# Variances ahead of the bonus products, attention scaled tile by tile, and part of w_out's operand splits ahead of the meeting

## The reference, cut to what matters

```python
def rwkv7_time_mix(...):            # 6 heads of 64
    ...
    _, y = lax.scan(step, s0, xs)   # the recurrence over 1024 tokens
    ym = y.mean(-1, keepdims=True)
    yv = jnp.square(y - ym).mean(-1, keepdims=True)
    yn = ((y - ym) * lax.rsqrt(yv + GN_EPS)).reshape(B, S, RWKV_WIDTH) * lnx_g + lnx_b
    bonus = (jnp.sum(r_h * k_h * r_k, -1, keepdims=True) * v_h).reshape(B, S, RWKV_WIDTH)
    return ((yn + bonus) * g).astype(zb.dtype)

def hybrid_mixer(...):
    ...
    o_a = rms_norm(o_a, attn_norm_g)          # attention, width 384
    o_b = rwkv7_time_mix(...)                 # width 384
    o_c = multiscale_pool(zc, pool_w, pool_scale)   # width 256
    return jnp.concatenate([o_a, o_b, o_c], axis=-1) @ w_out
```

## Time and profile before

| | us |
|---|---|
| median of three runs | 3576.71 (3575.73 to 3585.78) |
| the profiled execution, its own time | 3576.34 |
| its span | 3574.3 |
| TensorE busy | 3274.0 (92%) |
| VectorE busy | 1913.2 (54%) |
| ScalarE busy | 1053.9 (29%) |
| GpSimd busy | 1146.4 (32%) |

### The profile page before, as it was taken

The page is one execution under the profiler, slowest core; times in us unless marked ns, Lnnn a source line. Parts: engine busy times, 40 slices in busy tenths (PEclk is TensorE's granted clock), DMA queues, the critical chain, the costliest instruction groups (busy, mean ns, idle before and its releaser), DMA issues.

```text
span 3574.3 us, 61403 instructions
## 1 busy us (share of the span) xinstructions
PE 3274.0 (92%) x23080; PEld 2373.5 (66%) x23080; DVE 1913.2 (54%) x3061; ACT 1053.9 (29%) x1857; POOL 1146.4 (32%) x952
## 2 busy tenths in 40 slices
PE   7989967999999999999989998689899999999997
PEld 3444435876577888888735444368675788888884
DVE  5788996444623333333467899854526133333335
ACT  3333334442212211211235343344402111221212
POOL 1175632641212222222114755155222122222221
PEclk9999979999999999999999899799999999999998
DMA  3110000001111111111111001000011111111111
GB/s 123 45 33 21 29 23 6 0 1 36 48 36 48 47 47 47 53 47 48 40 55 33 28 24 33 11 6 0 7 31 58 42 51 49 47 47 47 48 46 47
DMA packets 43861, 132.72 MB, mean 37 GB/s; under 512 B 9280, under 2 KB 11840, under 8 KB 43072
## 3 DMA queue, kind: packets, MB, share of 16 engines
q1 hardware_dynamic: 37280, 122.41, 10.5%
q10 hardware_dynamic: 6432, 8.40, 0.9%
HBM read 117.15 MB, written 5.24 MB: 34 GB/s over the span
## 4 chain that ended last, share of the span: by engine, by line
PE 59%; DVE 14%; issue 10%; DVEq 10%; POOLq 2%; ACT 1%; POOL 1%; DMA 1%; PEldq 0%; ACTq 0%; SPq 0%; PEld 0%
DVE M L1715 8%; DVEq L1719 8%; PE wide L1087 7%; PE bank L1089 7%; PE bank L1087 7%; PE bank L1088 7%; PE wide L1089 7%; PE wide L1088 7%; PE wide L799 3%; DVE PB L1735 2%; PE wide L629 2%; PE bank L799 2%; POOLq L1591 1%; DVE WK L1717 1%; DVEq L1716 1%
## 5 line engine op out<-in xcount | busy, mean ns | idle before, releaser
L1590 POOL TENSOR_TENSOR WL<-WR,WH 128x1024 fp32r<-128x1024 f32 x160 | 403.1, 2519 | 1479.2 <-ACT WH L1385 1478.5
L669 PE MATMUL wide<-X,WR 128*128 128x512 f32 (+1 forms) x1088 | 504.7, 608 | 11.6 <-ACT X L1144 9.4
L1385 ACT ACTIVATE WH<-WR 128x1024 fp32r<-128x1024 f32 x160 | 168.2, 1053 | 735.6 <-PE bank L1089 430.2
L2019 DVE TENSOR_TENSOR RB<-RB 128x512 f32<-128x512 f32 x128 | 88.5, 692 | 549.0 <-ACT RB L1411 549.0
L669 PEld LDWEIGHTS wide<-X,WR 128*128 128x128 f32 x1088 | 202.7, 196 | 246.9 <-issue 220.9
L1715 DVE MAX8 M<-WK 128x8 f32<-128x512 f32 (+5 forms) x342 | 314.9, 921 | 23.7
L1717 DVE MATCH_REPLACE8 WK<-M,WK 128x512 f32<-128x512 f32 (+5 forms) x342 | 309.5, 905 | 1.2 <-issue 1.2
L1087 PE MATMUL wide<-XH,WH 128*128 128x512 f32 x640 | 261.6, 409 | 18.1 <-POOLq L1591 9.5
L1087 PE MATMUL bank<-XH,WH 128*128 128x512 f32 x640 | 255.7, 400 | 0.0
L1089 PE MATMUL wide<-XH,WL 128*128 128x512 f32 x640 | 252.8, 395 | 0.0
L1088 PE MATMUL wide<-XL,WH 128*128 128x512 f32 x640 | 252.5, 395 | 0.0
(11 more groups left out here) (318 smaller groups left out, 6399.2 us busy)
## 6 DMA issues: line engine op xcount, KB each, us to landing
WR<-in_w SPq DMA_DIRECT2D x128, 512.0 KB, 3.5
WR<-in_w_in SPq DMA_DIRECT2D x34, 512.0 KB, 3.5
WR<-in_w_out SPq DMA_DIRECT2D x16, 512.0 KB, 3.5
WR<-in_w_gate SPq DMA_DIRECT2D x16, 512.0 KB, 5.5
Y<-in_xT SPq DMA_DIRECT2D x2, 2048.0 KB, 13.3
out_T<-X SPq DMA_DIRECT2D x1, 4096.0 KB, 11.1
QZS<-QZ ACTq DMA_DIRECT2D x48, 64.0 KB, 2.0
QZS<-QZ ACTq DMA_DIRECT2D x64, 48.0 KB, 1.9
```

The lines of the kernel that those rows point to most:

```text
L669: mm = e.matmul(BK_[hf][:, 0:q.stop - q.start], WR[:, i % RING, kt, :], X[:, kt, q], start=kt == 0, stop=kt == KT - 1)
L1385: e.activation(WH[:, split_seq(i) % 2, :, :], WR[:, i % RING, :, :], ACT.Copy).then_inc(w_high, 1)
L1590: e.tensor_tensor(WL[:, s, :, :], WR[:, i % RING, :, :], WH[:, s, :, :].bitcast(F32), ALU.subtract)
L2019: e.tensor_tensor(RB[:, b, :], RB[:, b, :], RB[:, b, :], ALU.mult).then_inc(square_ready, 1)
```

## The change

The tail and the first steps of the projection are ordered anew.
- `var` moves ahead of all `bonus` entries in `post_seq`, and its matmuls take each half slab as soon as it is squared. Bonus 1 and 2 move behind the spreads; VectorE's list follows.
- ScalarE makes the copies for bonus 1 and 2 together behind the last squares.
- `scale_attention` works on one tile of 128 tokens and runs in `rwkv_tile`, between the last `XS` and the first `MT` of each tile.
- The slabs are taken in the order `M_ORDER` = 6, 0, 1, 2, 3, 4, 5, 7. The high parts of four of them (one pooling, three attention), the low parts of two and both parts of w_out's first block are made ahead of meeting 2; `LOW_AT` says where a low part lies in `ML`.
- Two pads move `G4` and the weights' high and low parts in SBUF, so that what is now written early lies on nothing that is still in use.

```diff
+M_ORDER = [6, 0, 1, 2, 3, 4, 5, 7]
+M_EARLY, M_AHEAD = 4, 2
+LOW_AT = [3, 4, 5, 0, 1, 2, 6, 7]
+G4_PAD, W_PAD = 4109, 819
...
+        sb("under_g4", [P, G4_PAD], post)
         G4 = sb("G4", [P, 3, S], post)
...
+        sb("under_wh", [P, W_PAD], m)
         WH = sb("WH", [P, 2, KT, P], m, F32R)
...
-        post_seq = [("mean", 0), ("mean", 1), ("mean", 2), ("bonus", 0), ("var", 0), ("bonus", 1), ("bonus", 2),
-                    ("spread", 0), ("spread", 1), ("gate", 0), ("spread", 2), ("gate", 1), ("gate", 2)]
+        post_seq = [("mean", 0), ("mean", 1), ("mean", 2), ("var", 0), ("bonus", 0), ("spread", 0), ("spread", 1),
+                    ("bonus", 1), ("gate", 0), ("spread", 2), ("bonus", 2), ("gate", 1), ("gate", 2)]
...
+            def variances(L):
+                for i in range(NP):
+                    for hf in range(2):
+                        e.wait_ge(y_sq, L * 6 + (2 * i + hf + 1))
+                        bank = post_bank(("var", 0), hf)
...
+                            mm = e.matmul(bank[:, c:c + 2], G1[:, i, q:q + P], block_ones[:, 0:P:HD],
...
-                post_read(e, L, ("gate", 0), 0)
+                post_read(e, L, ("spread", 2), 0)
                 keep_clock(2, 4)
                 meet(e, L, 2)
...
                     dense(mt, ZW + mt, lambda kt: kt, MH, ML,
...
+                          if mt == 0 else None, order=M_ORDER, low_at=LOW_AT)
...
+                def split_mixed(L, n0, n1):
+                    for kt in M_ORDER[n0:n1]:
+                        if kt < NP:
+                            e.wait_ge(att_scaled, L * NB + NB)
+                            e.wait_ge(bonus_in, L * 3 + (kt + 1))
+                        e.activation(MH[:, kt, :], mixed[kt], ACT.Copy).then_inc(m_high, 1)
...
+                    for k in ((0,), (), (1, 2))[i]:
+                        e.activation(G3[:, k, :], BZ[:, BR + k, :], ACT.Copy, scale=par_col("rk", k))\
+                         .then_inc(bonus_half, 1)
+                split_mixed(L, 0, 2)
                 split_high(L, ZW)
...
+                split_mixed(L, 2, M_EARLY)
...
                 meet(e, L, 2)
+                split_mixed(L, M_EARLY, KT)
...
                     e.tensor_tensor(G3[:, i, :], G3[:, i, :], BZ[:, BK + i, :], ALU.mult).then_inc(bonus_in, 1)
+                split_low(ZW)
                 meet(e, L, 2)
...
-            def scale_attention():
+            def scale_attention(t):
+                q = tile_columns(t)
                 for p in range(3):
...
+                    ins = e.scalar_tensor_tensor(A3[:, p, q], A3[:, p, q], par_col("ag", p), RSD[:, q], ALU.mult, ALU.mult)
+                ins.then_inc(att_scaled, 1)
...
                 for i in range(NP):
                     centre(i)
-                bonus(0)
-                scale_attention()
-                for i in range(1, NP):
-                    bonus(i)
+                lows(0, M_AHEAD)
                 for hf in range(2):
                     post_read(e, L, ("var", 0), hf)
...
                 e.reciprocal(g2, g2).then_inc(y_rstd, 1)
+                bonus(0)
                 normalise(0)
                 normalise(1)
+                bonus(1)
                 gated(0)
                 normalise(2)
+                bonus(2)
                 gated(1)
                 gated(2)
                 meet(e, L, 2)
-                for kt in range(KT):
...
+                lows(M_AHEAD, KT)
```

More of the change, by code:

```diff
@@ L971, in head_sums @@
                 return mm
+            def variances(L):
[3 more added lines that the diff above has]
+                        bank = post_bank(("var", 0), hf)
+                        for t in range(NB // 2):
+                            c, q = (i * (NB // 2) + t) * 2, hf * HALF + t * P
+                            mm = e.matmul(bank[:, c:c + 2], G1[:, i, q:q + P], block_ones[:, 0:P:HD],
+                                          start=True, stop=True)
+                        if i == NP - 1 and hf == 0:
+                            mm.then_inc(post_full, 1)
+                return mm
             def head_spread(bank, values, i, hf):
@@ L1058, in _ @@
                         if what == "var":
-                            e.wait_ge(y_sq, L * 6 + (2 * (NP - 1) + hf + 1))
-                            mm = head_sums(post_bank((what, i), hf), G1, hf)
+                            if hf == 0:
+                                variances(L).then_inc(post_full, 1)
+                            continue
                         elif what == "spread":
@@ L1070, in _, with dense @@
                         mm.then_inc(post_full, 1)
-                post_read(e, L, ("gate", 0), 0)
+                post_read(e, L, ("spread", 2), 0)
                 keep_clock(2, 4)
                 meet(e, L, 2)
-                def dense(n, i, ws, high, low, kts=KT, f=0, ready=None, halves=(0, 1)):
+                def dense(n, i, ws, high, low, kts=KT, f=0, ready=None, halves=(0, 1), order=range(KT), low_at=range(KT)):
                     e.wait_ge(w_low, L * N_SPLIT + f * N_F + (split_seq(i) + 1))
@@ L1082, in dense @@
                         e.wait_ge(d_free[b], L * D_USES + f * (N_DENSE // 2) + (n // 2 + 1))
-                        for kt in range(kts):
+                        for k, kt in enumerate(order[:kts]):
                             if ready:
-                                ready(kt, hf)
+                                ready(k, hf)
                             w, q = ws(kt), hs(hf)
-                            e.matmul(BK_[b], WH[:, s, w, :], high[:, kt, q], start=kt == 0, stop=False)
-                            e.matmul(BK_[b], WH[:, s, w, :], low[:, kt, q], start=False, stop=False)
-                            mm = e.matmul(BK_[b], WL[:, s, w, :], high[:, kt, q], start=False, stop=kt == kts - 1)
+                            e.matmul(BK_[b], WH[:, s, w, :], high[:, kt, q], start=k == 0, stop=False)
+                            e.matmul(BK_[b], WH[:, s, w, :], low[:, low_at[kt], q], start=False, stop=False)
+                            mm = e.matmul(BK_[b], WL[:, s, w, :], high[:, kt, q], start=False, stop=k == kts - 1)
                         mm.then_inc(d_full[b], 1)
@@ L1592, in split_low @@
                     e.drain().then_inc(w_used, 1 + GAP * (i == MLP0 - GAP - 1))
-                for i in range(ZW, MLP0 - GAP):
+                for i in range(NP):
+                    e.wait_ge(bonus_half, L * 3 + (i + 1))
+                    settle(e)
+                    e.tensor_tensor(G3[:, i, :], G3[:, i, :], BZ[:, BK + i, :], ALU.mult).then_inc(bonus_in, 1)
+                split_low(ZW)
+                meet(e, L, 2)
+                for i in range(ZW + 1, MLP0 - GAP):
                     split_low(i)
```

62 lines of the change are left out of this document (28 added, 34 removed).

## The result

The changed kernel takes 3606.18 us (median of 4 executions, 3602.49 to 3612.74). The kernel before took 3579.45 beside it (3575.73 to 3585.78). The ratio is 1.0075, 95% interval 1.0051 to 1.0099: slower by about 27 us, where 15 us less was forecast. The profiled execution took 3612.74, the longest of the four, and its span is 3610.7.

The account below looks back on a forecast made before the run. The prediction took the tail's chain of waits, through the reciprocal, meeting 2 and VectorE's low parts, as the bound. Gains of 1.9 + 5.55 us per layer, 14.9 in all, gave 3561.8 against 3576.71; 8-in-10 range 3555.5 to 3567.5.

Parts of the forecast that it names:

- the sum: Both layers' tails: 1.9 us up to the meeting plus 5.55 behind it, 7.45 per layer, 14.9 in all.
- The loop at nothing: Loop tiles ahead of `MT`: three scaling operations, 0.3 us each, fit VectorE's 4.80 us idle time and cost 0.
- The reciprocal 9.2 us behind the last `centre`'s end: Tail: the reciprocal ends at 808.75 instead of 815.63, 6.9 us earlier, with `centre` ending at 799.57.
- Rival A: Tail: GpSimd goes ahead of VectorE's low parts, the reciprocal ends 2.33 us later; 3565.6 to about 3568; 12%.
- Reciprocal to meeting: Tail: TensorE's spreads, bonuses, gates and keep_clock put the meeting 18.7 us behind the reciprocal; 1.0 us for the clock.
- The meeting's gain: Tail: meeting 2 comes 1.9 us earlier per layer, ends 0.9 and 2.9.
- Behind the meeting 9.35: Projection's first half tile: slab 7 ends 9.35 us behind the meeting, before 14.9, a gain of 5.55.
- The clock behind the meeting: Projection's start: despite TensorE's short waits the granted clock stays at 2.4 GHz, as a row at 842 to 843 showed.
- rival B: Behind the meeting the clock falls, losing 3.4 us per layer in the second half tile; 8.1 gained, 3568.6; 8%.
- the forecast's own sign of being wrong: Projection's second half tile: a granted clock of 0.5 there would show the forecast wrong.
- Rival C: Behind the meeting slab 7 comes ahead of `WL` and the clock stays up: 21.6 us gained, 3555.1; 10%.
- Rival D: Loop: the moved scaling reaches the recurrence's path, each tile late by 1.5 us, 24 in all; 3585.8; 4%.

Follow-up runs that it names:

- e5: The changed kernel with the pad ahead of `WH` raised from 819 to 1024 words (shift 4096 bytes) and `ST8` ahead of `LP`: 3563.17 us, ratio 0.9953.
- e4: The kernel before with only the attention's scaling, and the drain it needs, moved into the loop's tiles: 3577.36 us, ratio 0.9999.
- e11: e5 with one wait added, so GpSimd's low part of w_out's second block comes after VectorE's last low part: 3556.1 us, ratio 0.9933 to the kernel before.
- e18: The kernel before with 8 words behind `WR`, moving all tiles but `WR` and the constants by 32 bytes: 3578.86 us, ratio 1.0009.
- e10: The kernel before with 8 words between `WH` and `WL`, moving `WL` and what lies behind by 32 bytes: 3623.89 us (median of three), ratio 1.0123.
- e13: The kernel before with `WH` moved by 32 bytes, `WL` and everything behind it by 256: 3614.84 us, ratio 1.0100.
- e1: The kernel before with only the 819-word pad ahead of `WH` added (3296 bytes): 3620.06 us, ratio 1.0118.
- e16: The kernel before with `HH`, `HL` moved by 32 bytes and `Y`, `WH`, `WL` and all behind by 256: 3600.07 us, ratio 1.0068.
- e17: The kernel before with `HH`, `HL`, `Y`, `WH`, `WL` and all behind moved by 32 bytes: 3605.79 us, ratio 1.0088.

## Why the prediction was wrong

The direction was wrong; the step that failed is the sum. It took 3576.34 minus the tail's gain, and with that all work outside the tail at its old price, 7680 dense matmuls among it. The term for moving `WH` and `WL` was missing, no row of the kernel before could show it, and no rival had it. It is +47 us by TensorE's busy time, +43 by the comparison of the changed kernel with e5 (3606.18 - 3563.17). The description of the change names the pads as moves in SBUF, and the prediction gave them no price.

Point by point:

- The loop at nothing: right. The three operations took 0.87 us together, 0.3 each, and VectorE's idle time ahead of `MT` fell from 4.80 to 4.01, with 23.33 us from tile to tile as before. e4 confirms it. VectorE's timeline shows it:

```profile
737.11 0.87 DVE L1845 SCALAR_TENSOR_TENSOR A<-A,PAR,RSD  x3
741.99 0.62 DVE L1883 TENSOR_TENSOR MT<-wide,MT 128x192 f32<-128x192 f32 x2 [4.01 <-PE wide L879]
```

- The reciprocal 9.2 us behind the last `centre`'s end: right. It was 810.78 - 801.79 = 9.0, with the turns as forecast (product 3 ends at 809.33, low part 0 then, the reciprocal behind it). Rival A did not come. One reason was off: the variances took 7.95 us where the forecast had 6.55 at most, with the granted clock at 0.50 from 804 on, and the second square root waited 0.17 us for them.
- Reciprocal to meeting, 18.7 at the full clock and 1.0 for a low one: 831.03 - 810.78 = 20.25. The size was nearly right, the path was not. In the first layer the reciprocal doesn't hold TensorE up at all. The chain goes from the variances (to 809.01) to bonus 0, which the forecast had left out of this sum: its four matmuls take 3.62 us at a granted clock of 0.50 (1.98 in the earlier trace rows for four at the full one), and the first spread starts at 812.63, 1.85 behind the reciprocal. The meeting's gain was 1.58 (31.51 before, 29.93 now, from the last `centre`'s start) against 1.9. In the second layer bonus 0 was done in time and the meeting came 18.86 behind the reciprocal's end at 2580.01; there the gain was 2.99. The forecast had 0.9 to 2.9.
- Behind the meeting 9.35: 9.26. Right, `WL` came ahead of slab 7 as said.
- The clock behind the meeting: the sum went by the earlier trace rows, a short idle stretch that left it at 1.00, and rival B said that it falls. B was right in part, and so the forecast's own sign of being wrong, a granted clock of 0.5 in the projection's second half tile, was there. In the changed kernel:

```profile
838.00:840.00 2.00, 0.00 (x0) 0.00 (x0) 2.00 (x1) 0.00 (x0) 1.15 (x1) 1.00 0.00 0
...
841.00:842.00 1.00, 1.00 (x4) 0.81 (x3) 0.40 (x1) 0.00 (x0) 0.00 (x0) 0.50 0.57 233
```

TensorE was idle for 2.33 us ahead of the last triple (840.29), and from 840.93 to 843.92 its matmuls start every 0.43 us instead of 0.23. That loses 1.6 us, and as much in the second layer, where rival B had 3.4 per layer. The Trainium skill ("TensorE: Matmul & The Clock Gate", section "A second HAM failure mode: psum-queue depth-cycling") says that short idles between groups of matmuls can make the gate swing; by that rule the trace agrees for the idle stretch of 2.33 us, and e11 with idles of 0.17 us shows no swing; in the kernel before the rule and the trace differ, since an idle stretch nearly as long left the clock up (TensorE's timeline there):

```profile
844.19 0.50 PE L1087 MATMUL wide<-MH,WH 128*128 128x512 f32 x1 [2.24 <-DVE ML L1993]
```

What decides between the two is open.
- The tail as a whole, by the rows of the changed kernel: 7.25 + 8.66 - 2 x 1.6 = 12.7; 3576.34 - 12.7 + 46.7 = 3610.3, against 3612.74 in the profiled execution, the longest of its four. With the place repaired (e5) the medians give 15.0 of the forecast 14.9, but that agreement is partly luck: the interval reaches from 12 to 22 us, and by the changed kernel's rows a larger gain than forecast and a loss by the clock that the sum did not have cancel in part.
- Rival C, slab 7 ahead of `WL` and the clock up, was priced at 3555.1. It didn't come by itself; e11, which forces that order, took 3556.1.
- Rival D, slower by the recurrence: the sign came, the mechanism didn't (e4).

What stays open: why the distance counts. The runs show that it is between the streamed operand and the weights, that one weight block off its place makes neighbouring matmuls slow, and that multiples of 256 are free and 32, 64, 128 and 224 (modulo 256) are not. 96, 160 and 192 were not tried, nor a 16-bit type; plain fp32 matmuls lost nothing at 32 bytes (e18). A conflict between two reads of TensorE from SBUF, the stream and the load of the next weights, would fit the largest loss in e10, that of the matmul ahead of the one with `WL`. It does not by itself account for `HH,WH` at 395 ns in e10, where neither this matmul's weights nor the next one's are off, and it was not shown. `WH` alone cost 35 us (e13) and `WL` alone 46 (e10); the intervals of the two ratios overlap a little, and why they should differ is open.

## What to carry to other kernels

A pad, or a new tile ahead of old ones, is part of a change and has a price: before and after any edit of the allocation compare the number of matmul starts in a stretch where TensorE never waits. For fp32r matmuls keep the distance in bytes between the weights and each operand streamed against them at a multiple of 256, here worth 43 us of 3606. And when a change loses although its own stretch of the trace gained, look for one instruction form that is a little slower everywhere: a few nanoseconds on thousands of matmuls outweigh microseconds at a meeting.

## What the runs showed of the hardware

- fp32r matmuls of 128x512 start every 0.2268 us with the distance at a multiple of 256 bytes and every 0.2331 us at the distance of the changed kernel (224 modulo 256; 32, 64 and 128 the same within 0.001), at a granted clock of 1.00; their own duration goes from 389 to 395 ns. The busy time of the weight loads does not change (PEld 2373.5 us before, 2374.5 after). Plain fp32 matmuls of the same shape keep their 615 ns with the distance 32 bytes off (614, e18).
- The Trainium skill ("SBUF — State Buffer", section "Who interferes with whom") gives TensorE one read port for the moving operand and an independent one for the weights, and says that TensorE never waits on anyone. By that rule the place of a tile could cost nothing. The measurement decides: e1 changes only the place and takes 1.18% longer, and e16 and e17 tie it to just these two operands.
- A VectorE operation of two SBUF inputs that comes while GpSimd works waits for the end of that instruction and then goes first (3.37 us instead of 1.14 at 807.05), though GpSimd had `WL` queued, which then took 3.33 us (2.40 alone, in e11).
- The clock fell to 1.2 GHz behind an idle stretch of 2.33 us (changed kernel; 2.34 in e5), stayed at 2.4 GHz with gaps of 0.17 us (e11), and stayed there behind an idle stretch of 2.24 us in the kernel before.
